# Lower parts of the late gate weights, made in pieces of 256 columns in the projection, stored to HBM and loaded by the mixers

## What is computed

```python
proj = h @ w_in
offs = np.cumsum(IN_SPLITS)[:-1].tolist()
(gq, gk, gv, g_low, gr, hq, hf, hi, hg, sz, sxbc, sdt, gates) = jnp.split(proj, offs, axis=-1)
...
g = jax.nn.sigmoid(gates.astype(f32)).reshape(bsz, t_len, N_BRANCHES, D_MODEL).astype(dtype)
merged = (g[:, :, 0] * (y_gla @ w_br_gla)
          + g[:, :, 1] * (y_hgrn @ w_br_hgrn)
          + g[:, :, 2] * (y_ssm @ w_br_ssm))
```

## Time and profile before

| | us |
|---|---|
| median of 3 runs | 2038.89 (2036.88 to 2039.36) |
| profiled execution, span | 2040.4 |
| projection's steps, about | 182 to 528 |
| mixers, about | 577 to 1090 |
| TensorE busy in the span | 1925.7 |
| VectorE busy in the span | 1472.5 |
| ScalarE busy in the span | 1048.0 |

### The profile page before, as it was taken

How to read it: one execution, slowest core, us unless ns; L and a number is a source line. 1 busy time by engine, 2 the same in 40 slices (tenths; PEclk the granted TensorE clock), 3 DMA queues, 4 the chain that set the end, 5 groups by cost and what they waited for, 6 DMA issues and landing times. The chain is left out here.

```text
span 2040.4 us, 26797 instructions
## 1 busy us (share of the span) xinstructions
PE 1925.7 (94%) x10602; PEld 1576.7 (77%) x10603; DVE 1472.5 (72%) x1687; ACT 1048.0 (51%) x1234; POOL 218.3 (11%) x173
## 2 busy tenths in 40 slices
PE   6999999999999999999998999995999999999993
PEld 5789888888977777777776888874788888888881
DVE  5876467667227888788775656556889988999875
ACT  5234344444224545444444334223777887888763
POOL 3310000000030000000001000012122222222210
PEclk9999999999999999999998999997999999999996
DMA  5242332432355557656537654543999999999986
GB/s 168 86 145 73 114 104 97 131 104 93 107 145 158 151 160 168 167 127 152 160 115 282 206 204 182 229 178 138 349 376 384 389 386 385 389 386 387 387 331 259
DMA packets 212415, 436.11 MB, mean 214 GB/s; under 512 B 28018, under 2 KB 151042, under 8 KB 184770
## 3 DMA queue, kind: packets, MB, share of 16 engines
q1 hardware_dynamic: 179394, 355.68, 50.3%
q10 hardware_dynamic: 20864, 53.49, 7.5%
q0 software_dynamic: 12032, 25.22, 3.2%
HBM read 369.67 MB, written 81.43 MB: 221 GB/s over the span
## 5 line engine op out<-in xcount | busy, mean ns | idle before, releaser
L1602 PE MATMUL psum<-h_hi,l_hi 128*128 128x512 f32 x384 | 158.5, 413 | 4.9 <-PEq L58 3.3
L1602 PE MATMUL psum<-h_lo,l_hi 128*128 128x512 f32 x384 | 159.8, 416 | 0.0
L1602 PE MATMUL psum<-h_hi,l_lo 128*128 128x512 f32 x384 | 157.9, 411 | 0.0
L2741 DVE TENSOR_TENSOR gu_lo<-up_raw,gu_hi 128x2048 fp32r<-128x2048 f32 x64 | 146.3, 2288 | 13.2 <-ACT gu_hi L2684 13.2
L2684 ACT CAST gu_hi<-up_raw 128x2048 fp32r<-128x2048 f32 x64 | 122.1, 1909 | 35.0 <-PE u_ps L2813 35.0
L1258 ACT COPY l_out<-psum 128x512 f32<-128x512 f32 x48 | 28.1, 585 | 170.3 <-PE psum L1602 162.3
L2457 PE MATMUL mpsum<-y_hi,wb_hi 128*128 128x512 f32 x256 | 103.3, 403 | 10.1 <-DVE y_lo L2217 9.1
L2813 PE MATMUL g_ps<-gu_hi,xeT_hi 128*128 128x512 f32 x256 | 105.0, 410 | 5.8 <-DVE xeT_lo L2750 5.8
L806 DVE TENSOR_TENSOR w_lo<-w_raw,w_hi 128x512 fp32r<-128x512 f32 x90 | 61.9, 689 | 65.5 <-ACT w_hi L662 65.5
L662 ACT CAST w_hi<-w_raw 128x512 fp32r<-128x512 f32 x90 | 55.7, 622 | 91.9 <-PE ps L931 91.4
L2457 PE MATMUL mpsum<-y_lo,wb_hi 128*128 128x512 f32 x256 | 101.7, 397 | 0.0
(11 more groups left out here) (465 smaller groups left out, 5419.0 us busy)
## 6 DMA issues: line engine op xcount, KB each, us to landing
up_raw<-moe SPq DMA_DIRECT2D x62, 1024.0 KB, 8.1
gate_raw_a<-moe SPq DMA_DIRECT2D x33, 1024.0 KB, 8.4
gate_raw<-moe SPq DMA_DIRECT2D x33, 1024.0 KB, 8.4
dn_raw_a<-moe SPq DMA_DIRECT2D x31, 1024.0 KB, 7.2
dn_raw<-moe SPq DMA_DIRECT2D x31, 1024.0 KB, 8.0
w_raw<-w_in SPq DMA_DIRECT2D x26, 1024.0 KB, 6.1
l_raw<-w_gates ACTq DMA_DIRECT2D x24, 512.0 KB, 5.4
s_gates<-l_out ACTq DMA_DIRECT2D x48, 256.0 KB, 4.0
```

What stands on the lines that cost most here:

```text
L1602: ins = nc.tensor.matmul(psum[:, bank, :], w[t % 2][:, k, :], x[:, k, half * 512:half * 512 + 512], start=i == 0, stop=i == LATE_MM - 1, s ...
L2741: nc.vector.tensor_tensor(gu_lo[p][:], gu_raw[p][:], gu_hi[p][:].bitcast(F32), ALU.subtract).then_inc(gu_ready, 1)
```

## The change

`project` now makes the lower parts of the tiles 2 to 23. Each tile's 1024 columns are taken in four pieces of 256, 88 in all. SyncE loads a piece into one of three new buffers `l_piece` and stores the result to a new array `s_late_lo` in HBM; ScalarE casts it to its upper part, in a place at the end of the ring w_hi, and VectorE subtracts in the buffer. Step n of the projection handles six pieces (`PIECES_A_STEP`), each behind `upper(n + 1, i)` and `lower(n + 1, i)`. In the mixers VectorE's subtraction is gone; ScalarE's `late_hi` issues a load of `l_lo` from `s_late_lo` ahead of the cast, TensorE waits for the cast and for that load, and `late_load` waits for ScalarE's cast instead of VectorE's subtraction. The upper parts are still made in the mixers.

```diff
+LATE_T = WIDTHS["gates"] // P
+LATE_PIECE = 256
+LATE_PIECES = (LATE_T - 2) * KT * P // LATE_PIECE
+PIECES_A_STEP = 6
...
+        piece_hi = [rings[0][:, G * S + b * LATE_PIECE:G * S + (b + 1) * LATE_PIECE] for b in range(2)]
+        piece = [sb(f"l_piece{b}", [P, LATE_PIECE], F32R) for b in range(3)]
...
+            def load_piece(p):
+                if p >= LATE_PIECES:
+                    return
+                if p >= 3:
+                    sp.wait_ge(piece_out[p % 3], 16 * (p // 3))
+                sp.dma_start(piece[p % 3][:].bitcast(F32), piece_of(io["w_gates"][2:LATE_T], p)).then_inc(piece_in[p % 3], 16)
+
+            def store_piece(p):
+                sp.wait_ge(piece_lo_ready, p + 1)
+                sp.dma_start(piece_of(dr["late_lo"], p), piece[p % 3][:].bitcast(F32)).then_inc(piece_out[p % 3], 16)
+
             for t in range(1, len(COLS)):
+                if t == 4:
+                    load_piece(0)
+                    load_piece(1)
+                if t >= 5:
+                    for p in range((t - 5) * PIECES_A_STEP, min((t - 4) * PIECES_A_STEP, LATE_PIECES)):
+                        store_piece(p)
+                        load_piece(p + 2)
                 if t >= 3:
                     sp.wait_ge(prepared, t - 2)
...
+            def late_upper(n, i):
+                p = n * PIECES_A_STEP + i
+                if i >= PIECES_A_STEP or p >= LATE_PIECES:
+                    return
+                act.wait_ge(piece_in[p % 3], 16 * (p // 3 + 1))
+                if p >= 2:
+                    act.wait_ge(piece_lo_ready, p - 1)
+                nc.scalar.copy(piece_hi[p % 2], piece[p % 3][:].bitcast(F32)).then_inc(piece_hi_ready, 1)
...
+            def late_lower(n, i):
+                p = n * PIECES_A_STEP + i
+                if i >= PIECES_A_STEP or p >= LATE_PIECES:
+                    return
+                dve.wait_ge(piece_hi_ready, p + 1)
+                tt(piece[p % 3][:], piece[p % 3][:].bitcast(F32), piece_hi[p % 2].bitcast(F32), ALU.subtract).then_inc(piece_lo_ready, 1)
...
             def late_load(t):
                 if t >= 4:
-                    act.wait_ge(l_split, t - 3)
+                    act.wait_ge(l_hi_ready, t - 3)
...
             def late_hi(t):
+                act.wait_ge(l_done, 2 * (t - 2) + 2)
+                act.dma_start(l_lo[t % 2][:].rearrange("p k n -> p (k n)").bitcast(F32), dr["late_lo"][t - 2]).then_inc(lo_loaded[t % 2], 16)
                 act.wait_ge(l_loaded[t % 2], 16 * (t // 2))
-                act.wait_ge(l_done, 2 * (t - 2) + 2)
...
                         if t >= 2:
-                            pe.wait_ge(l_split, t - 1)
+                            pe.wait_ge(l_hi_ready, t - 1)
+                            pe.wait_ge(lo_loaded[t % 2], 16 * (t // 2))
```

More of the change, by code:

```diff
@@ L574, in project @@
         late_hi_ready = sem("late_hi_ready")
+        piece_in = [sem(f"piece_in{b}") for b in range(3)]
+        piece_hi_ready = sem("piece_hi_ready")
+        piece_lo_ready = sem("piece_lo_ready")
+        piece_out = [sem(f"piece_out{b}") for b in range(3)]
         dve_own = sem("dve_own")
@@ L594, in row_free, with piece_of @@
             eng.wait_ge(stored[n % 2], 16 + 32 * (n // 2))
+        def piece_of(ap, p):
+            t, q = divmod(p, KT * P // LATE_PIECE)
+            return ap[t][:, q * LATE_PIECE:(q + 1) * LATE_PIECE]
         tap_col = lambda n, a, k: taps[:, convs(n) % 2 * 2 + a, k:k + 1]
@@ L612, in _ @@
                                  .rearrange("(a p) k -> p a k", p=P)).then_inc(taps_loaded[q % 2], 16)
+            for b in range(3):
+                sp.wait_ge(piece_out[b], 16 * ((LATE_PIECES - b + 2) // 3))
         def loaded(eng, t):
@@ L839, in step @@
                 lower(m, 0)
+                late_lower(n, 0)
                 tap(n - 1, 0, 2)
                 lower(m, 1)
+                late_lower(n, 1)
                 summed(m, 1)
@@ L857, in step @@
                 lower(m, 5)
+                late_lower(n, 5)
                 lower(m, 6)
@@ L1041, in mixers @@
         l_hi_ready = sem("l_hi_ready")
-        l_split = sem("l_split")
+        lo_loaded = [sem(f"lo_loaded{b}") for b in range(2)]
         l_done = sem("l_done")
@@ L1371, in _ @@
             stt = nc.vector.scalar_tensor_tensor
-            def late_lo(t):
-                dve.wait_ge(l_hi_ready, t - 1)
-                tt(l_lo[t % 2][:], l_raw[t % 2][:], l_hi[t % 2][:].bitcast(F32), ALU.subtract).then_inc(l_split, 1)
-            def late(h):
-                if h % 2 and h // 2 + 2 < LATE_T:
-                    late_lo(h // 2 + 2)
             nc.vector.memset(eps[:], EPS).then_inc(eps_ready, 1)
@@ L1500, in body @@
                     gla_hgrn_out(c - 1)
-                else:
-                    late(3)
                 scores_in(0)
@@ L1513, in body @@
                     z_gated(c - 1)
-                    late(h0 - 1)
                 dve.wait_ge(bb_loaded, 16 * (c + 1))
@@ L1520, in body @@
                 factors(4)
-                late(h0)
                 dve.wait_ge(cb_ready, c + 1)
@@ L1529, in body @@
                 factors(5)
-                late(h0 + 1)
                 scores_in(4)
@@ L1552, in body @@
                 dec(i0 + 10)
-                late(h0 + 2)
                 dve.wait_ge(small_ready, c + 1)
@@ L1558, in body @@
                 tt(yt[:], inter_ps.rearrange("p (k t) -> p k t", t=CH), eb_in[:], ALU.mult).then_inc(inter_used, 1)
-                late(h0 + 3)
                 dve.wait_ge(upd_ready, c + 1)
@@ L1568, in _ @@
                 dec(i)
-            late(1)
             for c in range(NCH):
@@ L1577, in _ @@
             gla_hgrn_out(LAST)
-            for h in range(PREFIX + PER_CHUNK * NCH - 1, LATE_H):
-                late(h)
             ssm_out(LAST)
```

9 lines of the change are left out of this document (8 added, 1 removed).

## The result

| | median us | runs | profiled span |
|---|---|---|---|
| before, run beside it | 2038.1 | 4 (2036.88 to 2039.36) | 2040.4 |
| changed | 2048.5 | 4 (2044.37 to 2053.72) | 2052.0 |

The ratio is 1.0049, 95% interval 1.0032 to 1.0065: slower by 10.4 us (6.5 to 13.2). The forecast was 2048.0, +9.0.

A forecast was written before the change was run, and what follows sets the result against it. TensorE was taken to be busy throughout the projection and to have stalls in the mixers. Terms +4.7 (projection), +5.9 (first lower part) and -1.6 (chunks) sum to +9.0 on 2038.9, giving 2048 us; range 2031 to 2059.

The forecast's parts named there:

- The projection, +4.7: In even projection steps from 4 on, pieces delay VectorE's third addition and ScalarE's snapshot, so TensorE waits: +4.7 us.
- The first lower part, +5.9: At the mixers' start, half 4 waits 5.8 us for tile 2's load behind a slow store, then slow clock: +5.9 us.
- Chunks 1 to 7, -1.6: In the mixers' chunks, gains from the removed subtractions are mostly offset by later broadcast loads and slow clock: -1.6 us.
- The price of a neighbour: In the chunks, a 512 KB load lengthens the broadcast by 1.3 us if ahead of it, 0.7 if issued during it.
- The bound of -12: Lower bound for the mixers' chunks if the transfers don't contend: -12 us.
- Rival A: Transfers don't get in each other's way: half 4 doesn't wait, chunks gain 11.8 us, total 2031.8 us; chance 0.18.
- Rival B: First lower part comes in time, but broadcasts are lengthened as forecast: 2042.0 us, no measurable change; chance 0.22.
- Rival C: Projection's piece loads and stores take 3.9 us or more each, late pieces hold ScalarE and VectorE: 2062 us; chance 0.12.

The follow-up runs named there:

- e1: The change's projection, making and storing pieces, with the mixers of the kernel before (subtraction on VectorE, no loads of lower parts): 2043.4 us, ratio 1.0024.
- e11: The change, with the pieces' casts and subtractions in the projection made by GpSimd in place of ScalarE and VectorE: 2055.0 us, ratio 1.0074.
- e3: The kernel before with neither subtraction nor load of lower parts in the mixers, so later tiles' lower parts are wrong: 2028.6 us, ratio 0.9953.
- e2: The projection work of the kernel before with the change's mixers, loading one stored tile of zeros 22 times: 2048.2 us, ratio 1.0045.
- e4: The change, with the first two late tiles' lower parts again subtracted on VectorE and loads only from tile 4 on: 2044.0 us, ratio 1.0036.
- e5: The change, with three pieces instead of six in even projection steps from 4 on, spreading pieces up to step 17: 2049.8 us, ratio 1.0056.
- e7: e6 with VectorE's `cbm` moved ahead of its wait for the broadcast load in each chunk: 2031.7 us, ratio 0.9962 against the kernel before.
- e12: e3 with `cbm` moved ahead of the wait for the broadcast, lower parts of tiles 2 to 23 neither made nor loaded: 2013.5 us, ratio 0.9890.
- e6: The change with both edits of e4 and e5, first two late tiles on VectorE and pieces spread: 2047.2 us, ratio 1.0042.
- e9: The kernel before with the late tiles' subtraction in the mixers made by GpSimd in place of VectorE: 2031.2 us, ratio 0.9955.
- e10: The kernel before with the subtraction on GpSimd and `cbm` ahead of the wait for the broadcast: 2024.5 us, ratio 0.9916.

## Why the prediction was right, point by point

- *The projection, +4.7.* Measured +4.8 in the change and +5.1 in e1. Forecast were five waits of 0.84 and one of 0.50; there are five of 0.94 to 0.97 and one of 0.61. Mechanism and place hold: the third addition late by the pieces that no gap takes up, ScalarE's chain behind it, the snapshot. That the delay starts with VectorE and not with ScalarE's own casts is in the two lines of 361.33 and 362.05 above, and e11 agrees: without a piece on ScalarE the snapshot is late all the same.
- *The first lower part, +5.9.* Measured +6.2. The landing was forecast at 608.4, 30.7 us after the mixers' first matmul; it came 31.0 after it (617.97 - 586.93). The wait was 6.05 for 5.8, the slow clock followed, and 2.0 us were absorbed for 1.5. The row chosen, the store of 14.8 us in the same queue, was the right neighbour: the median of the 22 loads is 5.4 us and would have given no wait at all. Its parts hold too. Counted from the mixers' first matmul, the stretches of the earlier trace rows are 601.2 to 613.2 and 613.2 to 617.2 here: 80 GB/s flow and then 370, for 84 and 337. The store took 14.9 us, and the load behind it landed 1.6 us after it, for 1.5. Not foreseen were the 2.30 us that pass in ScalarE's issue of the load; they lay inside the wait for the landing.
- *Chunks 1 to 7, -1.6.* Measured -1.9. The terms as written add up to -1.5, not -1.6. The sum is right, its parts are not, and that they cancel is luck. Chunk 1 gained 1.8 (forecast 0.95). Chunk 2, forecast to gain 0.44, lost 3.4, since its broadcast took 20.1 us, against 16.0 before. Chunk 3 lost 1.3 instead of gaining 1.9, chunk 4 gained 2.9 (forecast 0.44), chunk 5 gained 1.5 instead of losing 2.0, chunk 6 gained 0.6, and chunk 7 nothing (forecast 0.95). The price of a neighbour holds in the sum: 2.0 for each of four odd chunks and 0.7 for each of three even ones make 10.1 us over the seven broadcasts, and they grew by 7.9. Single landings scatter by more than a neighbour costs.
- *The bound of -12* for no contention came from instructions ahead of the stall; e3 gave -10.9 in chunks 1 to 7 (423.8 against 434.7).
- *Rival A* (2031.8) is out: the first part landed late and the broadcasts were longer. The Trainium skill, "DMA: Bandwidth & Descriptors", section "Queues, rings and completion order", which stood beside it, has the DMA engines take turns between queues. That may be so packet by packet, which no run here shows, but a load of 512 KB in ScalarE's queue still took 16.2 us beside SyncE's loads of the chunk's start, three times its median. *Rival B* needed the first lower part in time; e2 and e4, where its wait comes and goes, show that it isn't. *Rival C* is out: the loads of pieces took 2.7 us in the middle and their stores 1.8, not 3.1. A late piece does hold the queues where C says (32.7 us), but only the spread of e5 to e7 put such a wait where it reached TensorE.
- *Not in the working:* what issuing costs ScalarE. The 22 issues of `l_lo` took

```profile
L1310 ACTq DMA_DIRECT2D l_lo<-s_late_lo x22: 444/465/3664, 601.8 to 1065.0; - x22
```

17.4 us in all, three of them 1.2 to 3.7 us. So two thirds of the 26.8 us that left VectorE came back on ScalarE, whose squares, evictions and `rs` TensorE waits for in e4 and e7. In e7 TensorE's waits for ScalarE are 7.4 us, in e12 0.6, of 10.5 us between their mixers. Whether the issues or the broadcasts' later landing (121.5 us against 113.0) make ScalarE late there was not separated.

What stays open: what makes the waits and the slow clock fall differently in the same mixers (4.7 us between e4 and e6); how often the first stage has its slow stretch of 4 us; and where the rest of the 10 us lies by which single runs of one kernel differ. With one profiled execution for each kernel, a difference of mixers under some 5 us is not established by the stages alone. The sign of the change itself, and those of e1 to e12, rest on the medians and their intervals.

## What to carry to other kernels

Before work is moved to shorten a stall, look at which instruction ends it and at what that one itself needs: here it stood behind a wait for data that it never reads, and moving it took 13 us off the mixers of the profiled execution and 5.6 off the median, where moving the subtractions had put 4 on the mixers and, with the projection, 10.4 on the median. Price a transfer by the rows of the same queue at the same time of the program, not by its median, and count its issue on the engine that makes it. If an idle engine can do the work in place, try that before HBM: the same 22 subtractions on GpSimd gained 9 us, though in a stage without slack (e11) the same engine cost 6.

## What was unexpected in the hardware

- *VectorE beside GpSimd.* In e9 several of VectorE's instructions with two operands in SBUF grew (554 to 593 ns, 352 to 442), others did not (`q_lv` of 384 columns 555 and 551, though 669 in e10); those with one operand in PSUM did not (686, 684). In e11 689 grew to 802, and the additions with an operand in PSUM stayed at 690 and 688. GpSimd's subtraction grew too, from 2.40 us in the projection of before to 2.60. The Trainium skill, "SBUF — State Buffer", section "Who interferes with whom", says just that: a VectorE instruction with two SBUF inputs contends with a GpSimd instruction that reads SBUF, since its second input comes through the read interface that both share. The trace agrees in kind; which instructions met a GpSimd one in time was not followed one by one.
- *A DMA issue is not always short.* The same instruction on ScalarE's queue took 0.44 to 3.66 us (the line above); the long ones lie where broadcasts and other loads were under way. In e7 one held ScalarE for 3.06 us:

```profile
737.06 3.06 ACTq L1322 DMA_DIRECT2D l_lo<-s_late_lo  x1
740.17 1.04 ACT L1324 CAST l_hi<-l_raw 128x1024 fp32r<-128x1024 f32 x1 [3.50 <-issue]
```

- *A stall is dearer than its length.* Behind TensorE's wait of 6.05 us the matmuls ran at the granted clock of 0.50 for 3 us, behind that of 5.50 until 762, 4 us after it; behind the waits of 1 us in the projection none did. In between it is not the length alone that decides: of the seven stalls of 2.39 to 2.80 us in the chunks of the kernel before, five have 3.4 us at the granted clock of 0.50 beside them, and two of 2.39 and 2.41 us (chunks 5 and 7) have none.
